# HGRN levels and inputs as separate threads on VectorE and ScalarE

## The reference, cut to what matters

```python
bcum = jnp.cumsum(gc, axis=1)
total = bcum[:, -1]
new_state = jnp.exp(total)[..., None] * state + jnp.einsum(
    'bshk,bshv->bhkv', kc * jnp.exp(total[:, None] - bcum), vc)
decay = jnp.exp(jnp.where(causal, bcum[:, :, None] - bcum[:, None], -jnp.inf))
scores = jnp.einsum('bthk,btshk,bshk->bhts', qc, decay, kc)
o = jnp.einsum('bhts,bshv->bthv', scores, vc) + jnp.einsum(
    'bthk,bhkv->bthv', qc * jnp.exp(bcum), state)
```

## Time and profile before

| what | value |
|---|---|
| time, median of 3 runs | 3563.51 us (3563.43 to 3565.44) |
| profiled execution, its own time | 3567.69 us |
| its span | 3565.8 us |
| instructions | 37968 |
| TensorE busy | 3389.7 us, 95% of the span |
| VectorE busy | 1474.7 us, 41% |
| ScalarE busy | 1051.3 us, 29% |
| GpSimd busy | 338.4 us, 9% |
| mean granted TensorE clock | 0.977 |

### The profile page before, as it was taken

One profiled execution on the slowest core, in us unless ns is written; L12 is line 12 of the kernel. 1 busy time (PEld: TensorE's weight loads), 2 busy tenths in 40 slices (PEclk: granted clock), 3 DMA queues, 4 the chain that ended last, 5 costly groups with the idle time before them and its releaser, 6 DMA issues. The chain is left out here.

```text
span 3565.8 us, 37968 instructions
## 1 busy us (share of the span) xinstructions
PE 3389.7 (95%) x16472; PEld 2563.3 (72%) x16472; DVE 1474.7 (41%) x2049; ACT 1051.3 (29%) x1515; POOL 338.4 (9%) x322
## 2 busy tenths in 40 slices
PE   6999999989899999999998989999998999999999
PEld 3445556666667888888886766788886888888887
DVE  5245434566443211113337342455643443333333
ACT  4222222443332211112115553333323322222211
POOL 1000002333213000000003000021221100000000
PEclk9999999999999999999999999899998999999999
DMA  5111110000013111112122010000003111111211
GB/s 231 41 59 48 60 60 15 24 12 12 13 71 136 53 48 48 48 42 85 47 76 86 24 37 28 7 1 1 1 1 133 56 48 48 48 48 36 101 43 70
DMA packets 35254, 182.29 MB, mean 51 GB/s; under 512 B 4261, under 2 KB 4261, under 8 KB 21648
## 3 DMA queue, kind: packets, MB, share of 16 engines
q1 hardware_dynamic: 22176, 133.18, 10.5%
q0 software_dynamic: 12912, 46.69, 3.4%
HBM read 161.89 MB, written 17.96 MB: 50 GB/s over the span
## 5 line engine op out<-in xcount | busy, mean ns | idle before, releaser
L525 PE MATMUL ps<-r,r 128*128 128x512 f32 x2656 | 1056.7, 398 | 14.4 <-DVE r L1988 13.1
L527 PE MATMUL ps<-r,r 128*128 128x512 f32 x2656 | 1048.0, 395 | 0.0
L526 PE MATMUL ps<-r,r 128*128 128x512 f32 x2656 | 1047.9, 395 | 0.0
L525 PEld LDWEIGHTS ps<-r,r 128*128 128x128 f32 x2656 | 501.4, 189 | 142.3 <-issue 20.8
L526 PEld LDWEIGHTS ps<-r,r 128*128 128x128 f32 x2656 | 501.6, 189 | 117.2 <-issue 3.2
L527 PEld LDWEIGHTS ps<-r,r 128*128 128x128 f32 x2656 | 501.3, 189 | 115.7
L515 PE MATMUL ps<-ar 128*128 128x128 f32 (+7 forms) x2228 | 448.1, 358 | 7.0 <-DVE ar L1992 3.3
L515 PEld LDWEIGHTS ps<-ar 128*128 128x128 f32 (+3 forms) x2228 | 274.6, 177 | 166.1 <-issue 139.8
L1394 ACT ACTIVATE ar<-ps 128x512 f32<-128x512 f32 (+3 forms) x336 | 173.2, 540 | 719.5 <-PE ps L627 169.9
L1981 DVE TENSOR_TENSOR r<-ar,r 128x1024 fp32r<-128x1024 f32 (+1 forms) x170 | 204.6, 1204 | 325.0 <-ACT r L1356 324.9
L1356 ACT ACTIVATE r<-ar 128x1024 fp32r<-128x1024 f32 (+1 forms) x170 | 174.4, 1033 | 551.8 <-PE ps L527 510.9
(11 more groups left out here) (274 smaller groups left out, 3291.7 us busy)
## 6 DMA issues: line engine op xcount, KB each, us to landing
ar<-in_w_mod SPq DMA_DIRECT2D x24, 1024.0 KB, 4.9
ar<-in_w_gu SPq DMA_DIRECT2D x22, 1024.0 KB, 4.9
ar<-in_w_up SPq DMA_DIRECT2D x22, 1024.0 KB, 4.8
ar<-in_w_in SPq DMA_DIRECT2D x19, 1024.0 KB, 4.9
ar<-in_w_dn SPq DMA_DIRECT2D x32, 512.0 KB, 3.5
x<-ar POOLq DMA_DIRECT2D x48, 256.0 KB, 2.3
ar<-x POOLq DMA_DIRECT2D x24, 512.0 KB, 7.3
ar<-in_xT POOLq DMA_DIRECT2D x16, 512.0 KB, 14.0
```

The source lines that it names most:

```text
L525: M.matmul(o, whk, hi[k][:, a:a + n], start=k == 0, stop=False)
L526: M.matmul(o, whk, lo_[k][:, a:a + n], start=False, stop=False)
L527: ins = M.matmul(o, wlk, hi[k][:, a:a + n], start=False, stop=k == nk - 1)
```

## The change

On VectorE and ScalarE `direction(hh, d)` is cut into two generators, `inputs` and `levels`, which keep the turns that their operations had. A round now takes `levels` of direction 0, `levels` of direction 1, then `inputs` of both, then the feed. In a turn of a level VectorE's copies of the level before now stand ahead of the level's product. The programs of TensorE, GpSimd and SyncE are as before. In the diff ScalarE's program comes first, then VectorE's.

```diff
-            def direction(hh, d):
+            def inputs(hh, d):
...
-                yield
-                yield
+                for _ in range(15):
+                    yield
+                if hh < 3:
+                    gate_exp(hh + 1, d)
+                yield
+                yield
+                if hh < 3:
+                    gate_log(hh + 1, d)
+                yield
+
+            def levels(hh, d):
+                for _ in range(12):
+                    yield
                 for lv in range(1, 8):
                     x = (t1s, Xs)[lv % 2][d][:, 0:1024]
                     act.wait_ge(*p_gate.at(("xd", hh, d, lv)))
                     A.activation(x, x, ACT.Exp).then_inc(*a_gate(("x", hh, d, lv)))
                     yield
-                    if lv == 7 and hh < 3:
-                        gate_exp(hh + 1, d)
-                    yield
-                yield
-                if hh < 3:
-                    gate_log(hh + 1, d)
-                yield
+                    yield
+                yield
+                yield
...
-            together(heads(0), heads(1), feed())
+            together(heads(0, levels), heads(1, levels), heads(0, inputs), heads(1, inputs), feed())
...
                 ins.then_inc(*v_state(("s", hh, d)))
-                yield
-                for lv in range(1, 8):
-                    L, fs, fq = level_block(d, lv)
-                    xq = blk((t1s, Xs)[lv % 2][d], L)[:, :, fq, :]
-                    dve.wait_ge(*a_gate.at(("x", hh, d, lv)))
-                    V.tensor_tensor(xq, xq, blk(q, L)[:, :, fq, :], ALU.mult).then_inc(*v_gate(("x", hh, d, lv)))
-                    if lv > 1:
-                        level_done(lv - 1)
-                    yield
-                    yield
-                level_done(7)
-                yield
+                for _ in range(16):
+                    yield
                 if d:
                     dve.wait_ge(*product.at(("ho", hh, 1)))
...
+            def levels(hh, d):
+                for _ in range(12):
+                    yield
+                for lv in range(1, 8):
+                    L, fs, fq = level_block(d, lv)
+                    xq = blk((t1s, Xs)[lv % 2][d], L)[:, :, fq, :]
+                    if lv > 1:
+                        level_done(hh, d, lv - 1)
+                    dve.wait_ge(*a_gate.at(("x", hh, d, lv)))
+                    V.tensor_tensor(xq, xq, blk(qs[hh % 2], L)[:, :, fq, :], ALU.mult).then_inc(*v_gate(("x", hh, d, lv)))
+                    yield
+                    yield
+                level_done(hh, d, 7)
+                yield
+                yield
...
-            together(heads(0), heads(1), feed())
+            together(heads(0, levels), heads(1, levels), heads(0, inputs), heads(1, inputs), feed())
```

More of the change, by code:

```diff
@@ L1561, in direction, with heads @@
                     yield
-                    if lv == 7 and hh < 3:
-                        gate_exp(hh + 1, d)
                     yield
                 yield
-                if hh < 3:
-                    gate_log(hh + 1, d)
                 yield
-            def heads(d):
+            def heads(d, part):
                 for _ in range(15 * d):
@@ L1573, in heads @@
                 for hh in range(4):
-                    yield from direction(hh, d)
+                    yield from part(hh, d)
             for part in parts_of(0)[:5]:
                 block(0, *part)
-            together(heads(0), heads(1), feed())
+            together(heads(0, levels), heads(1, levels), heads(0, inputs), heads(1, inputs), feed())
         def mixed(tag, k, a):
@@ L2148, in feed, with level_done, inputs @@
                     yield
-            def direction(hh, d):
+            def level_done(hh, d, lv):
+                for half in range(2):
+                    key = ("sc", hh, d, lv, half)
+                    dve.wait_ge(*product.at(key))
+                    dst = th(Sc[d][:, half * 512:half * 512 + 512])
+                    if lv == 0:
+                        if hh:
+                            dve.wait_ge(*product.at(("ho", hh - 1, d)))
+                        mk_ = IDN.rearrange("p (c t) -> p c t", c=1).to_broadcast([128, 4, 128])
+                        V.tensor_tensor(dst, th(bank(key)), mk_, ALU.mult).then_inc(*v_state(key))
+                    else:
+                        dve.wait_ge(*v_state.at(("sc", hh, d, lv - 1, half)))
+                        m0 = (7 * d + lv - 1) * 128
+                        mk_ = masks[:, m0:m0 + 128].rearrange("p (c t) -> p c t", c=1).to_broadcast([128, 4, 128])
+                        V.copy_predicated(dst, mk_, th(bank(key))).then_inc(*v_state(key))
+            def inputs(hh, d):
                 z, q, t1b, g, kk = zs[hh % 2][d], qs[hh % 2], t1s[d], gs[d], kks[d]
                 bc, kt, ktT, tot, S0 = z, g, t1b, tots[d], S0s[d]
[L2154 to L2168, removed]
                 def scan(chunks):
@@ L2193, in direction @@
                 V.tensor_tensor(kk, bc, kk, ALU.subtract).then_inc(*v_gate(("bk", hh, d)))
-                level_done(0)
+                level_done(hh, d, 0)
                 yield
```

## The result

The changed kernel takes 3538.18 us (median of four runs, 3535.4 to 3541.15) where the kernel before takes 3563.48 beside it: 0.9929 of it, 95% interval 0.9916 to 0.9941, 25.3 us less. In a second set of five runs it was 3543.44 against 3563.54, 0.9943 (0.9931 to 0.9956), 20.1 us less. So the sign was right, and the size was wrong by more than a factor of two in both sets. The profiled execution took 3537.5 against 3567.69.

A forecast was written before the change was run, and what follows sets the result against it. TensorE, busy 95% of the span, was taken as the bound, so gains come from its idle time or clock. 5.1 + 0.2 + 0.5 + 1.4 + 1.5 = 8.7 us off 3563.51 gave 3554.8; range of 8 in 10: 3542 to 3565.

The forecast's parts named there:

- The reading of the bound: TensorE is busy 95% of the span; only its idle time, some 46 us in the HGRN stretch, or its clock can give time.
- B: Direction 0's inputs, now behind direction 1's levels, become what TensorE waits for; 2.1 us stay, 3561.4; chance 0.28.
- D: Level products wait for GpSimd's pair, so levels start later; 20 of 40 losing 0.9 us gives 3574.3; chance 0.10.
- The tails: Direction 1's levels 4 to 7, then direction 0's level 1, in three heads: net 1.7 us gained per head, 5.1 in all.
- Direction 0's own levels: Level 3 gains 0.67, level 5 gives it back wholly or partly: 0.1 for each of two heads, 0.5 first, 1.4 last.
- its rule of copies before product: A level begins one copy, about 0.67 us, earlier if the exponential is late, one copy later if VectorE is.
- The clock in the levels: The half-speed stretch at 687.50 to 690.80, after TensorE's 2.48 us idle, counted as gone: 1.5 us.
- The clock elsewhere: Outside the HGRN stage no gain or loss was counted, since the change touches that stage alone.
- slow stretches in new places: Slow clock stretches in new places, listed as a sign of being wrong, with no size and no place given.
- Rival C: Waits on the copies go by half or more, clock included: 20 us of the 39.4 gives 3543.5; chance 0.10.

The follow-up runs named there:

- late_bk: The changed kernel with one small VectorE fill (128x256) ahead of direction 1's subtraction in heads 1 to 3; 3547.81 us, 0.9950 of the kernel before.

## Why the prediction was wrong

**The reading of the bound was right.** All gains lie in TensorE's idle time and clock. No other engine became the bound, and rivals B and D did not come: level 0 and the transposes wait for nobody in the tails.

**The tails: right in kind, a little small.** 4.89 us of waits a head (0.87, 1.42, 0.12, 2.48) became 2.60 (1.39, 1.21), a gain of 2.3 against the 1.7 forecast: level 7 was put at 1.7 and level 1 at 1.4 to 1.6. Three heads, 6.9 against 5.1. That both halves are needed for it is in none of its terms: it reckoned with both orders at once and did not price either alone.

**Direction 0's own levels: the step that failed.** "... the product behind two copies gives the 0.67 back, wholly or in part. I take 0.1 for each of two heads ..." Level 3 came as forecast (1.93 to 1.21). Level 5 did not give it back, it won 1.63 more, because VectorE's subtraction, some 0.5 us earlier against TensorE and GpSimd, came ahead of GpSimd's distances by 0.09 us instead of 0.43 behind. The prediction took both operations of this race as stretched as before. With new waits of 0.13 at level 4 and 0.41 at level 6, each of the two heads gained 1.8, outside the bounds of -0.6 to 1.3 that it gave. In the first head, where the race had been won already, level 5 went from 1.00 to 1.95, a loss, as its rule of copies before product says; the head's gain was 0.5 to 0.9 with the waits behind it, near the 0.5 forecast. The last head gave 1.4, as forecast.

The waits sum up to 12.3 to 12.9 us, where 7.2 were forecast: the sizes of the tails and of level 5 make up the difference.

**The clock in the levels: mis-sized.** 1.5 us were counted, for one slow stretch, and that stretch is gone in both profiles. Busy time of the same matmuls fell by 4.4 in one profile and by 0.9 in the other of the two pairs, so the term has the right order of size, and no single execution can give its number.

**The clock elsewhere: a term that was missing, and the largest.** The prediction put everything outside HGRN at nothing: "The change touches one stage alone, the HGRN one". That holds for the program and not for the time: the RWKV start got 9.4 us shorter, by its granted clock. The prediction named slow stretches in new places as what could make it wrong, in the direction of a loss, and gave them no term and no place in the range. Without this one the medians would have been some 3547.6 and 3552.8 (3538.18 and 3543.44 plus 9.4), an estimate, and inside the range.

**Rival C** had the right size, for the wrong reason: 11.1 of the 39.4 us of waits on the copies went, not half.

## What to carry to other kernels

When two engines with an in-order program feed a third, put the work that frees a buffer ahead of the work that waits for an operand; it costs one operation's length only where the engine itself is late. Waits that end within a tenth of a microsecond of another engine's start are no fixed prices: cost them from both sides of the race. Before a gain of a few tenths of a per cent is put down to an edit, compare the stages that the edit doesn't touch, and shift the rest of the kernel by a little work of no use to see whether a later stage's clock depends on when it begins.

## What the runs showed of the hardware

A stage of TensorE can take one of two times, 15.8 or 25.2 us here, the same one in both profiles of each of the two kernels that were profiled twice, and change between them when matmuls of some 2 us are added ahead of it, so that more work is less time (3563.69 to 3555.28). The TensorE clock was granted at 0.58 in the long one and 1.00 in the short one, after a row of dense matmuls and the same two waits of 0.8 us. Over thirteen profiles the length went with where the stage begins against the last rise of the clock ahead of it: 57.0 to 57.2 us behind that rise in the six long ones, and in none of the seven short ones. Why was not settled.

Of two operations of this stage, on VectorE and GpSimd, that both read two inputs from SBUF and overlap, one runs in its usual time and the other lasts as if it had begun behind the first: 1.47 and 2.75, or 2.42 and 1.50. The Trainium skill, page "SBUF — State Buffer", section "Who interferes with whom", tells this as an exclusive lock that goes to whoever issues first. The traces agree in the lengths. The starts in a profile do not always show who had it: GpSimd's distances are shown 0.03 us ahead of the product in the changed kernel (715.05 and 715.08) and in late_bk (716.79 and 716.82), and were stretched in the first and the product in the second. In late_bk GpSimd's operation at 712.87 was stretched as well, against a subtraction shown at 713.06; VectorE's fill had begun at 712.86, and whether the fill had a part in that no run here shows.
